# Token blocks of a first projection: products of 512 columns split into two halves of 256

## The reference

```
proj = rmsnorm(x, ab_norm_g) @ ab_w_in            # (1024 x 1024) @ (1024 x 6680)
z_a, xbc, dt, z_b, q, k, v, i, f, o = split(proj)
y = concat(ssd(xbc, dt, z_a), mlstm(q, k, v, i, f, o, z_b)) @ ab_w_out
x = x + y
```

## Time and profile before

| what | us |
|---|---|
| median of two runs | 1757.46 (1757.23 to 1757.69) |
| the profiled execution | 1758.6 |
| its span, first to last instruction | 1756.9 |
| TensorE busy | 1626.0 (93%) |
| mean granted TensorE clock | 0.962 of full |

### The profile page before, as it was taken

The page is one execution under the profiler, slowest core; times in us unless marked ns, Lnnn a source line. Parts: engine busy times, 40 slices in busy tenths (PEclk is TensorE's granted clock), DMA queues, the critical chain, the costliest instruction groups (busy, mean ns, idle before and its releaser), DMA issues. The chain is left out here.

```text
span 1756.9 us, 21081 instructions
## 1 busy us (share of the span) xinstructions
PE 1626.0 (93%) x8241; PEld 1334.7 (76%) x8241; DVE 743.1 (42%) x1260; ACT 532.0 (30%) x1129; POOL 275.7 (16%) x218
## 2 busy tenths in 40 slices
PE   6999999999999849999699975998999999999698
PEld 5888888888888538788588864787878887878586
DVE  5675541111110057777634315234554334564333
ACT  5221111111111123344322205224454432556321
POOL 3000000000000015555100004022122203222110
PEclk9999999999999969999799987998999999999899
DMA  4342223222211143343213033011111102112532
GB/s 145 134 156 96 96 94 110 96 96 96 97 52 48 39 152 100 134 156 126 96 48 121 24 119 119 18 34 57 60 49 54 43 7 79 37 49 66 217 119 96
DMA packets 112527, 155.29 MB, mean 88 GB/s; under 512 B 7174, under 2 KB 68746, under 8 KB 111418
## 3 DMA queue, kind: packets, MB, share of 16 engines
q1 hardware_dynamic: 112442, 154.13, 25.6%
HBM read 109.97 MB, written 44.14 MB: 88 GB/s over the span
## 5 line engine op out<-in xcount | busy, mean ns | idle before, releaser
L491 PE MATMUL p_bank<-p_w_hi,p_h_hi 128*128 128x512 f32 x512 | 199.2, 389 | 0.0
L491 PE MATMUL p_bank<-p_w_lo,p_h_hi 128*128 128x512 f32 x512 | 199.2, 389 | 0.0
L491 PE MATMUL p_bank<-p_w_hi,p_h_lo 128*128 128x512 f32 x512 | 199.2, 389 | 0.0
L2007 PE MATMUL a_ps<-a_h_hi,a_w_hi 128*128 128x512 f32 x384 | 163.9, 427 | 4.7 <-DVE a_h_lo L1807 4.7
L1837 DVE CUSTOM_DVE_ANT_0 a_s<-a_ps,a_neg_dist 128x256 f32<-128x256 f32 (+7 forms) x128 | 92.0, 755 | 148.8 <-PE a_ps L2025 148.8
L2007 PE MATMUL a_ps<-a_h_hi,a_w_lo 128*128 128x512 f32 x384 | 152.8, 398 | 0.0
L2007 PE MATMUL a_ps<-a_h_lo,a_w_hi 128*128 128x512 f32 x384 | 152.7, 398 | 0.0
L1616 POOL TENSOR_TENSOR a_w_lo<-a_w_raw,a_w_hi 128x1024 fp32r<-128x1024 f32 x40 | 95.1, 2380 | 319.5 <-DVE a_w_hi L1827 261.0
L1727 ACT ACTIVATE a_s<-a_s,a_nm 128x256 f32<-128x256 f32 (+7 forms) x128 | 98.3, 769 | 126.0 <-DVE a_nm L1837 125.9
L374 ACT ACTIVATE p_stage<-p_bank 128x512 f32<-128x512 f32 x64 | 38.3, 598 | 302.8 <-PE p_bank L491 302.8
L491 PE MATMUL p_bank<-p_h_hi,p_w_hi 128*128 128x512 f32 x320 | 125.5, 392 | 4.0 <-DVE p_h_lo L401 4.0
(11 more groups left out here) (311 smaller groups left out, 3126.8 us busy)
## 6 DMA issues: line engine op xcount, KB each, us to landing
p_w_raw<-in_ab_w_in SPq DMA_DIRECT2D x12, 2048.0 KB, 8.8
tok<-p_stage SPq DMA_DIRECT2D x64, 256.0 KB, 2.0
a_w_raw<-in_c_w_in SPq DMA_DIRECT2D x32, 512.0 KB, 4.0
k_gz<-tok SPq DMA_DIRECT2D x8, 1536.0 KB, 10.1
k_fe<-feat SPq DMA_DIRECT2D x8, 1280.0 KB, 6.7
y_w_raw<-in_ab_w_out SPq DMA_DIRECT2D x8, 1024.0 KB, 5.4
a_s<-x SPq DMA_DIRECT2D x12, 512.0 KB, 6.7
feat<-p_junk SPq DMA_DIRECT2D x10, 512.0 KB, 2.6
```

Of the source, the lines that this page charges most:

```text
L491: mm = pe.matmul(out, a, c, start=(q == 0), stop=(q == len(pairs) - 1))
L2007: mm = pe.matmul(o, x, y, start=(k == 0 and q == 0), stop=(k == KT - 1 and q == 2))
```

## The change

Each bank of a token block is filled in two halves: first 24 products on columns 0 to 255, then 24 on columns 256 to 511. The same stationary slices are used in both, and so are loaded twice. `full` is raised after the last product of the second half. Feature blocks and gates stay as they are.

```
                     ts = slice(o * P, (o + 1) * P)
-                    products(bank[o][:, :], [pair for k in range(KT) for pair in (
-                        (h_hi[:, k, ts], w_hi[par][:, k, :]), (h_hi[:, k, ts], w_lo[par][:, k, :]),
-                        (h_lo[:, k, ts], w_hi[par][:, k, :]))]).then_inc(full, 1)
+                    for c in (slice(0, BLK // 2), slice(BLK // 2, BLK)):
+                        mm = products(bank[o][:, c], [pair for k in range(KT) for pair in (
+                            (h_hi[:, k, ts], w_hi[par][:, k, c]), (h_hi[:, k, ts], w_lo[par][:, k, c]),
+                            (h_lo[:, k, ts], w_hi[par][:, k, c]))])
+                    mm.then_inc(full, 1)
```

## The result

The changed kernel takes 1779.7 us (median of two runs, 1779.69 and 1779.70) against 1757.46: 1.0117 times as long, with a 95% interval of 1.01 to 1.0133. The forecast was 1760.5 us, range 1754 to 1781. The number lies in the range, at its upper end, and 1.7 us from where the second case, a price paid per product, had been put: 1778 us. The likeliest case, 1756 to 1769 us, did not happen.

The account below looks back on a forecast made before the run. The prediction took TensorE to bound the kernel. Its terms, 0 + 0 + 2 + 1 = 3 us on the profiled 1758.6 us, gave 1761.6 us, then 1760.5 us since the runs' median is 1.1 us lower; range 1754 to 1781 us.

Parts of the forecast that it names:

- the second case: Token-block products on TensorE: a fixed start cost of some 6.7 ns each, adding 20.5 us, 1778 us; chance 0.20.
- The likeliest case: Token blocks on TensorE: splitting the products costs 0 to 11 us, total 1756 to 1769 us; chance 0.62.
- The bound: Token blocks, 247.0 to 595.5 us: TensorE alone sets the time, and each added nanosecond per product lengthens the kernel one for one.
- Streaming: Token-block products: time proportional to columns, so a half takes 113.3 ns and costs nothing; upper bound 120 ns, 20.5 us.
- Loading: Each half's weight load on TensorE: least step with its product 111.5 ns, hidden under 113.3 ns by 1.8 ns; no cost.
- The slower rival: The 3072 halves on TensorE: loads not hidden, 169 ns per half, 172 us more, 1930 us; chance 0.07.
- What rides along: Token loop on TensorE: bank waits, register steps and taken jumps no longer fully covered; 2 us plus 1 us.
- The 2 us for the bookkeeping of each bank: The 64 token-block banks: wait and register step exceed 0.09 us of cover; 0 to 9 us, taken as 2.
- The 1 us for the two jumps: The token loop's two taken jumps, with a body doubled in code: between 0 and 5 us, taken as 1.
- refetch: Token loop's jumps back: the doubled body is not kept, so each waits for packets; 5 us, 1764.5 us; chance 0.05.
- The fixed price per product: Token-block products: some 6.7 ns each beyond the proportional part, wherever the data goes; 20.5 us, 1778 us; chance 0.20.
- Quicker halves: Token-block halves: only the 111.5 ns load step remains, so 6 us less, 1752 us; chance 0.06.

Follow-up runs that it names:

- e1: The changed kernel with unequal parts of 384 and 128 columns instead of two of 256; 1849.99 us, against 1758.48 for the kernel before.
- e2: The changed kernel with unequal parts of 320 and 192 columns instead of two of 256; 1803.37 us, against 1758.48 for the kernel before.
- e7: The kernel before, 512 columns in the token blocks, with the first projection's high and low parts in bfloat16 instead of float32r; 1729.88 us.
- e8: The changed kernel, 256 columns in the token blocks, with the first projection's high and low parts in bfloat16 instead of float32r; 1734.50 us.
- e11: The changed kernel, 256 columns streamed, with only 64 tokens of each tile loaded in the token blocks; 1759.33 us.
- e12: The changed kernel, 256 columns streamed, with only 32 tokens of each tile loaded in the token blocks; 1771.35 us.
- e4: The kernel before, 512 columns streamed, with only the first 64 tokens of each tile loaded in the token blocks; 1764.38 us.

## Why the prediction was right or wrong

**The number.** The forecast added 3 us and the change cost 22. The range held because it was drawn wide enough to take in the second case; its own part, 1756 to 1769 us, was missed. That it stayed within two percent was forecast with 0.92 and came true, though by 20.5 us of a cost that the sum had at nothing.

**The bound.** Right. TensorE alone set the stage, and 20.5 of the 21.0 us by which the span grew are in it; the cost per product passed to the end one for one. VectorE's wait per block grew from 36.8 to 39.4 us, as spare time does:

```profile
DVE p_w_hi L431 <- PE p_bank L491: 230.7, 6, 39.4
```

**Streaming.** This is the step that failed, the new interval of a half: "I take 113.3, because the duration rows remove what pairing adds to the starts." A half took 120.0 ns and not 113.3, so the term was sized at nothing and measured 20.5 us. The earlier trace rows compared pairs of 64-row products, 390 ns against 276, and the difference of 114 ns looked proportional. Full-array products show 389 and 283 ns, a difference of 106 ns, which is 256 columns at 2.4 GHz and leaves the 13.3 ns in both. So the mean durations of paired products on 64 rows did not carry over to single ones on 128. The starts in the earlier trace rows, 115 to 120 ns apart, said the right thing and were set aside. One division would have warned: 226.7 ns is 13.3 more than 512 columns at the granted clock, and an excess like that needs a cause before it is halved.

**Loading.** Right in kind: the load needs 111 to 112 ns with its product (e1, e2) and stays hidden at 256 columns. The margin was 8 ns, not 1.8, because the stream itself was longer. The slower rival, loads that are not hidden, did not occur: even at 192 columns only the step of the load remained. (In its price, 2 x 169 - 226.7 is 111 ns and not 112, so 171 us.) A rule by which loads overlap only with other row groups was contradicted again at 256 columns; that was the Trainium skill's ("TensorE: Matmul & The Clock Gate", The mechanism), a section that also names a background weight buffer into which a load can go ahead, and against that the trace does not speak.

**What rides along.** The 2 us for the bookkeeping of each bank were 0: TensorE was busy for 369.50 of 369.50 us. Since records of 283 ns overlap, that alone would not show small gaps, but the timeline does: all 196 steps from 399.81 us on, over four banks, are 0.12 us. The sum asked how far the queue runs ahead if the issue of the instructions takes 111.5 ns; at 120.0 ns a product it had more room than that, and no cost showed. The 1 us for the two jumps was also 0, and no refetch came. The DMA queues of the changed kernel from 392 to 580 us, when passes two and three ran:

```profile
q8 instruction: 1, 0.02, 0.0%
q14 instruction: 2, 0.02, 0.0%
```

Over the whole span queue 8 moved

```profile
q8 instruction: 63, 1.03, 0.2%
```

where the page of the kernel before has 57 packets: six more, and one in these two passes. Code fetched anew at each jump would have come with every pass. The doubled body was kept, against the two-page window that the Trainium skill states ("Runtime: NRT & Kernel Launch", Instruction fetch mechanics). The same section gives TensorE's memory 2048 instructions, and the doubled body's 768 loads and 768 products fit into that; the trace agrees with this figure.

**The rivals.** The fixed price per product was given 0.20 and 1778 us; it is what the changed kernel shows, down to the sign named for it, intervals of 120 ns with no idle, and its bound of 120 ns from the earlier trace rows was exact. That bound was the longer of two values, 115 and 120 ns, read from starts with two digits, so its exactness is in part luck. Its mechanism was worded too widely ("wherever its data goes"): it holds for this format and for a full load only (e7, e8, e11, e12). Quicker halves did not occur in the change; the step of 111.5 ns, on which they rested, showed only at 192 and 128 columns.

## What to carry to other kernels

Where TensorE bounds a stage, do not split float32r products while the load is full: each product costs 13.3 ns on top of its columns, and the step of a load with its product, 111.5 ns, takes over at 192 columns and below (by an estimate from these two figures, below (111.5 - 13.3) x 2.4 = 236). Before extrapolating to a new width, write the measured step as columns over clock plus a rest, and treat the rest as paid per product until rows of the same shape say otherwise. Where two kinds of rows disagree, prefer distances between starts to modelled durations.

## What the runs showed of the hardware that was not expected

The extra time of a float32r product depends on both operands' widths in no simple way: 13.3 ns (128 loaded, 256 or 512 streamed), 6.7 (64, 256), 11.1 (32, 256), 16.7 (64, 512), 17.7 (24, 512). Loading less can be slower: e4 leaves half of the loaded columns out and takes 230.0 ns a product instead of 226.7. bfloat16 has 2.5 ns in its place, with load records of 0.10 us instead of 0.19; per 512 columns a product of that format follows 4.8% sooner.
